# Order of values, transposes, scores and gate tiles on TensorE within a step of the attention loop

## The reference

```
cq, ckv, kidx, widx, mq, mk, mv, ga, gb = split_cols(h @ w_in[i])
y_dsa = dsa_attention(...) @ w_proj_dsa[i]     # 8 heads, each query attends to its top 128 keys
y_moba = moba_attention(...) @ w_proj_moba[i]  # 8 heads, own causal block and past blocks
y = sigmoid(ga) * y_dsa + sigmoid(gb) * y_moba
# in each branch, per head:  s = q @ k - slope * dist, masked;  p = softmax(s);  o = p @ v
```

## Time and profile before

| | |
|---|---|
| median of 3 runs | 1139.06 us (1138.75 to 1142.0) |
| the profiled execution | 1140.5 us, span 1138.6 us |
| busy: PE, PEld, DVE, ACT, POOL | 1120.9, 910.2, 559.9, 502.7, 181.6 us |
| mean granted TensorE clock | 0.998 |
| the attention loop on PE | 520.85 to about 675 us of the span |

### The profile page before, as it was taken

How to read it: one execution, slowest core, us unless ns; L and a number is a source line. 1 busy time by engine, 2 the same in 40 slices (tenths; PEclk the granted TensorE clock), 3 DMA queues, 4 the chain that set the end, 5 groups by cost and what they waited for, 6 DMA issues and landing times.

```text
span 1138.6 us, 14794 instructions
## 1 busy us (share of the span) xinstructions
PE 1120.9 (98%) x5449; PEld 910.2 (80%) x5449; DVE 559.9 (49%) x904; ACT 502.7 (44%) x870; POOL 181.6 (16%) x114
## 2 busy tenths in 40 slices
PE   7999999999999999999999999999999999999998
PEld 5678888888888888877777788887888888888887
DVE  3544444544444465589984527677333333332232
ACT  5565656465444434245565554444233222322233
POOL 0055354444333501000000000040000000000000
PEclk9999999999999999999999999999999999999999
DMA  9845655665555224222221223322332332333221
GB/s 313 281 148 189 222 178 169 194 222 180 176 175 175 76 72 139 56 56 75 53 59 38 57 74 93 92 75 74 121 100 74 111 111 74 105 122 102 83 70 75
DMA packets 159100, 138.26 MB, mean 121 GB/s; under 512 B 3551, under 2 KB 157522, under 8 KB 159058
## 3 DMA queue, kind: packets, MB, share of 16 engines
q1 hardware_dynamic: 130948, 109.38, 31.0%
q10 hardware_dynamic: 28110, 28.32, 7.6%
HBM read 135.59 MB, written 2.10 MB: 121 GB/s over the span
## 4 chain that ended last, share of the span: by engine, by line
PE 94%; DVE 3%; ACT 2%; issue 0%; DMA 0%; ACTq 0%
PE ps L373 28%; PE ps L375 28%; PE ps L374 28%; PE ps L1192 2%; PE ps L1227 2%; PE ps L1205 1%; DVE w_lo L352 1%; PE ps L1034 1%; PE ps L504 1%; DVE nrm L430 0%; DVE h_lo L436 0%; PE ps L1150 0%; PE ps L656 0%; PE ps L654 0%; PE ps L655 0%; ACT prob L1392 0%
## 5 line engine op out<-in xcount | busy, mean ns | idle before, releaser
L352 DVE TENSOR_TENSOR w_lo<-raw,w_hi 128x1024 fp32r<-128x1024 f32 (+1 forms) x164 | 241.2, 1471 | 388.6 <-ACT w_hi L347 388.5
L373 PE MATMUL ps<-h_hi,w_hi 128*128 128x512 f32 x1008 | 399.2, 396 | 2.2 <-DVE h_lo L436 1.9
L375 PE MATMUL ps<-h_hi,w_lo 128*128 128x512 f32 x1008 | 393.5, 390 | 0.0
L374 PE MATMUL ps<-h_lo,w_hi 128*128 128x512 f32 x1008 | 393.0, 390 | 0.0
L347 ACT ACTIVATE w_hi<-raw 128x1024 fp32r<-128x1024 f32 (+1 forms) x164 | 183.7, 1120 | 368.8 <-PE ps L375 367.8
L373 PEld LDWEIGHTS ps<-h_hi,w_hi 128*128 128x128 f32 x1008 | 189.6, 188 | 49.2 <-issue 7.8
L375 PEld LDWEIGHTS ps<-h_hi,w_lo 128*128 128x128 f32 x1008 | 189.5, 188 | 40.3
L374 PEld LDWEIGHTS ps<-h_lo,w_hi 128*128 128x128 f32 x1008 | 189.7, 188 | 37.6 <-issue 0.2
L373 PE MATMUL ps<-g_hi,w_hi 128*128 128x512 f32 x330 | 129.8, 393 | 0.2 <-issue 0.2
L375 PE MATMUL ps<-g_hi,w_lo 128*128 128x512 f32 x330 | 128.6, 390 | 0.0
L374 PE MATMUL ps<-g_lo,w_hi 128*128 128x512 f32 x330 | 128.5, 389 | 0.0
(11 more groups left out here) (221 smaller groups left out, 1016.2 us busy)
## 6 DMA issues: line engine op xcount, KB each, us to landing
raw<-in_w_ffn SPq DMA_DIRECT2D x42, 1024.0 KB, 5.4
ada<-in_w_ada ACTq DMA_DIRECT2D x27, 1024.0 KB, 5.1
raw<-in_w_ffn SPq DMA_DIRECT2D x16, 1408.0 KB, 6.2
raw<-in_w_in SPq DMA_DIRECT2D x64, 256.0 KB, 3.2
ada<-in_w_ada SPq DMA_DIRECT2D x16, 512.0 KB, 8.8
raw<-in_w_out SPq DMA_DIRECT2D x16, 256.0 KB, 3.1
x_tok<-in_x SPq DMA_DIRECT2D x4, 512.0 KB, 4.7
raw<-in_w_ffn SPq DMA_DIRECT2D x8, 256.0 KB, 7.8
```

The source lines that it names most:

```text
L352: nc.vector.tensor_tensor(tiles_of(w_lo[j % SPL], nk), raw_of(f, j, nk), tiles_of(w_hi[j % SPL], nk).bitcast(F32), ALU.subtract).then_inc( ...
L373: nc.tensor.matmul(ps[:, bank, :], hi, rhs_hi, start=start, stop=False)
L374: nc.tensor.matmul(ps[:, bank, :], hi, rhs_lo, start=False, stop=False)
L375: return nc.tensor.matmul(ps[:, bank, :], lo, rhs_hi, start=False, stop=stop)
```

## The change

Before, PE's iteration m ran scores(m), values(m - 2), transposes(m - 1), gate tiles. Now, from step 2 on, it runs values(m - 2), transposes(m - 1), scores(m), gate tiles. Steps 0 and 1 keep their order. No other engine's list of work is changed, and no buffer or wait either.

```diff
             for m in range(NST + 2):
-                if m < NST:
+                if m < 2:
                     scores(m)
                 if m == 1:
                     value_tile(3)
                 if 2 <= m < NST + 2:
                     values(m - 2)
                 if 1 <= m < NST + 1:
                     transposes(m - 1)
+                if 2 <= m < NST:
+                    scores(m)
                 for i in gate_tiles[m]:
                     gate_tile(i)
```

## The result

The changed kernel takes 1145.97 us (median of 4 runs, 1145.33 to 1146.09), the kernel before, run beside it, 1139.09 (4 runs, 1138.75 to 1142.0). The ratio is 1.0053, with a 95% interval of 1.0041 to 1.0064: slower by half a per cent. The profiled execution took 1146.1 us with a span of 1144.2, where the sum gave 1146.0 and 1144.1.

What follows compares the result with a forecast made beforehand. The prediction took TensorE, busy 98% of the span, as the bound; 2.7 us of waits plus 2.8 us for the boundary made 5.5 us, taking the 1139.06 us median to 1144.5 us, range 1141.3 to 1148.0.

Steps and rivals of the forecast that it cites:

- the sum: Whole kernel: waits of 2.7 us plus boundary of 2.8 us, 5.5 us slower; profiled execution 1146.0 us, span 1144.1.
- The boundary: TensorE, transposes into scores, steps 2 to 15: a fourth tile-mode change costs 0.20 us a step, 2.8 us in all.
- The one row of step 1: Score load behind a transpose load at 529.55: 0.31 us against 0.11 into gates, giving the 0.20 us a step.
- the upper bound of 0.38: Highest price allowed for transposes into scores: 0.38 us a step, 5.3 us in all.
- The waits: TensorE before transposes in steps 2 to 6, waiting for DVE's normalised probabilities: 2.7 us in all.
- the walk: Step-by-step timing of TensorE against DVE's chain from scores to normalised probabilities, wake-up 0.15 us; gives 2.7 us of waits.
- (b): Rival: one of the two costs, boundary or waits for DVE, is absent; 1141.8 or 1141.9 us, chance 0.15.
- (c): Rival: value matmuls newly wait for ACT in seven even steps, 2.3 us more, 1146.8 us; chance 0.08.
- the margin: Before values in step 8: ACT's copies of transposes end 0.8 us before values need them.
- (d): Rival: faster, as gates hide the weight loads' idle time behind scores, 9.2 us back, 1135.4 us; chance 0.04.
- (e): Rival: the chain simply shifts at no cost, 1139.1 us; chance 0.03.

Runs made afterwards that it cites:

- e11: Kernel before, old loop, with the one-column token sums and kiw's four transposes spread between matmuls of the q projections' third unit; 1139.02 us, ratio 0.9983.
- e5: The changed kernel run again unaltered, beside the kernel before; 1145.83 us, ratio 1.0046.
- e3: Changed kernel with the select rounds of steps 2 to 6 left out, so its top-key mask is not the reference's; 1141.86 us, ratio 1.0020.
- e2: Changed kernel with the old order up to step 6 and the new order only from step 7 to 15; 1142.00 us, ratio 1.0017.
- e8: Kernel before, given e2's order, but with each step's first gate tile between transposes and scores from step 7; 1142.07 us, ratio 1.0014.
- e9: Kernel before, old order, with one gate tile moved between scores and values in steps 2 to 15; 1143.84 us, ratio 1.0026.
- e4: Changed kernel with scores moved between values and transposes, so values, scores, transposes, gates from step 2; 1139.92 us, ratio 1.0001.
- e7: Changed kernel with transposes moved ahead of values, so transposes, values, scores, gates from step 2; 1154.04 us, ratio 1.0116.
- e6: Changed kernel with select rounds dealt evenly, three in step 1 and two in each later step up to 7; 1145.07 us, ratio 1.0036.
- e1: Changed kernel with the new order in steps 2 to 6 only and the old order from step 7; 1143.79 us, ratio 1.0028.
- e10: e7 with select rounds dealt evenly as in e6; 1148.7 us, ratio 1.0067.

## Why the prediction was right

**The whole.** Predicted 5.5 us; the profiled loop lost 5.63, in a repeat 5.46. The median came out at 1145.97 for 1144.5, inside the range, and the 1.5 us are not in the steps but in the base: the sum was laid on 1139.06, while the 64 later runs of the kernel before had medians of 1140.1 to 1140.9. In the repeat the difference of medians was 5.3 us. What moves those runs is, at least in part and by e11, the half clock behind the token sums, which lasted a different time in different executions.

**The boundary, 2.8 us.** 2.87 us in the changed kernel by its own late steps (7 x 0.23 + 7 x 0.18), 2.6 in its repeat e5 by the same sum, 2.62 in e3, 0.19 to 0.21 a step in e2, e8 and e9. The one row of step 1 that carried it, 0.31 against 0.11 us, was no accident of that place, and the upper bound of 0.38 was too careful. But the row was right for a simpler reason than I gave. I priced the pair transposes to scores; e8 has no such pair and pays the same. The price goes with one more change of the kind of tile, and e4 shows the other side: an order with three changes is free (e7's, by its late steps, costs 0.04 us a step). The Trainium skill, "TensorEngine Tiling (Array Packing)", section "Key Properties", has changing the mode drain TensorE. By that rule the count decides, and these runs agree with it in sign and in place; it gives no duration, which here is 0.19 to 0.21 us a change.

**The waits, 2.7 us.** Against unwaited steps of 9.54 and 8.52 us:

| step | 2 | 3 | 4 | 5 | 6 | sum |
|---|---|---|---|---|---|---|
| predicted | 0.75 | 0.75 | 0.22 | 0.75 | 0.20 | 2.7 |
| measured | 0.69 | 0.68 | 0.41 | 0.88 | 0.05 | 2.7 |

The sum is exact by luck in part: steps 4 and 5 wait longer and step 6 less. Against the unwaited steps of the repeat, 9.49 and 8.53 us, its waits add up to 2.85. Starts came where the walk had them to within 0.25 us (scores(4) 560.57 for 560.47 measured, scores(8) 597.85 for 597.96). Three sizes in the walk were off. The wake-up of PE was 0.06 us and not 0.15; that step 2 came out within 0.01 us is luck, for DVE ran 0.1 us later than the walk had it. That takes some 0.08 us off each wait, about the miss of steps 2 and 3 and part of that of step 6. biased(4) began 1.95 us after the first score, not 1.60 (biased(6) 1.59), which lengthens step 4; why is open. And step 5 does not repeat step 3: rounds alternate between a search (L1593 before) and a replacement (L1595 before), step 3 has one replacement and step 5 two, and its chain from biased() to the reciprocal took 6.37 us (571.69 to 578.06) for 6.17. e3 and e6 show the cause, the selections and how they are dealt.

**The rivals.** (b) fell with e1 to e3: both costs are there, each without the other. (c) Once the loop ran, the value loads idled 0.35 us whether ACT (548.05) or "issue" (557.31) stands as releaser, so ACT did not hold them up; the margin held. (d) The weight loads' idle time of 0.54 and 0.76 us behind scores went with the scores: e2's and e3's steps are longer, not shorter. (e) fell with the result. I had scores to gates priced as scores to values, and that holds: 2.02 us from the first score in the changed kernel (541.04 to 543.06).

**What stays open.** The late even steps are 9.54 us in the changed kernel's profile and 9.49 in e2's and in e5's, which is the same kernel again; so this is a difference between executions, of the size of the 0.3 us by which e1 and e2 together stay under the change, and its cause is not known. The late biased(4). And the part of e7's and e10's loss beyond their walk that the 0.04 us a step does not cover.

## What to carry to other kernels

On a full TensorE, count the changes of tile kind (64 or 128 rows, 64 or 128 columns) in the loop before reordering it, and close the loop when you count: an order that keeps the count was free or nearly so, one more change costs about 0.2 us each time round here. Then take the distance on TensorE between a producer and the work that needs its result, and compare it with the producer's chain step by step, not with the engines' mean load: uneven dealing of the same 17 rounds made some two us of waiting. A price that rests on one row of the trace should be read as the cheapest rule that gives this row (a count), and tried at a place that has the rule and not the row.

## What the hardware showed that I had not expected

The granted clock of TensorE goes from 1.00 to 0.50 (2.4 to 1.2 GHz) inside a busy loop: in e7 after 2.04 and 2.24 us in which PE did nothing, and then while it was busy again. With idle times up to 1.3 us, in the changed kernel and in e10, it did not fall. It also fell without idle time in the records, behind the 12 matmuls of one column, up to 444 us in the kernel before and up to 447 in e5, and not at all in e4 and e10: the same instructions can meet it or not. With the 12 spread among wide matmuls (e11) the profile shows no fall, and 11 runs agree with that by their time. The Trainium skill, "TensorE: Matmul & The Clock Gate", section "Part 1: The HAM clock gate", says that the throttle knows a full and a half rate only and follows how busy the engine is; the windows of 1 us agree with the first (1.00 and 0.50, apart from those with an edge in them). With the second the stalls of e7 agree; the stretch of one-column matmuls, which the records show busy throughout, neither bears it out nor speaks against it. So a stall can cost more than its own length: in e7 about 1.7 us more for each of two.
